# Expert weights in 4 MB transfers instead of 2 MB, in five places instead of ten

## What is computed

```python
logits = jnp.einsum('btd,de->bte', h, router_w)
affinity = jax.nn.softmax(logits, axis=-1)
gate, idx = lax.top_k(jnp.swapaxes(affinity, 1, 2), capacity)      # capacity = 32 tokens per expert
xe = jax.vmap(lambda hb, ib: hb[ib])(h, idx)
hidden = silu(einsum('becd,edf->becf', xe, w_gate)) * einsum('becd,edf->becf', xe, w_up)
ye = einsum('becf,efd->becd', hidden, w_down) * gate[..., None]
out[idx] += ye
```

## Time and profile before

| what | value |
|---|---|
| median of 3 runs | 1953.06 us |
| the profiled execution's own time | 1951.2 us |
| its span, first to last instruction | 1949.4 us |
| TensorE matmul busy | 1521.6 us, 78% |
| VectorE, ScalarE, GpSimd busy | 624.6, 526.5, 133.8 us |
| moved by DMA | 542.00 MB |
| expert weights | 192 transfers of 2048 KB, 46.0 to 46.6 us from issue to landing |

### The profile page before, as it was taken

The page is one execution under the profiler, slowest core; times in us unless marked ns, Lnnn a source line. Parts: engine busy times, 40 slices in busy tenths (PEclk is TensorE's granted clock), DMA queues, the critical chain, the costliest instruction groups (busy, mean ns, idle before and its releaser), DMA issues.

```text
span 1949.4 us, 25931 instructions
## 1 busy us (share of the span) xinstructions
PE 1521.6 (78%) x11219; PEld 1032.8 (53%) x11237; DVE 624.6 (32%) x963; ACT 526.5 (27%) x864; POOL 133.8 (7%) x151
## 2 busy tenths in 40 slices
PE   7999999999999997899888656556565655665555
PEld 7888999887999797789564111111111111111111
DVE  4665544665444554445752000000000000000000
ACT  6445343545343556425631000000000000000000
POOL 0251000031000013410200000000000000000000
PEclk9999999999999988999999787887778788787787
DMA  9443555433555443213097999999999999999997
GB/s 270 140 146 121 187 192 178 148 131 128 174 193 177 136 128 112 86 47 130 1 388 316 426 429 427 427 428 427 428 428 427 427 428 427 428 428 428 427 429 324
DMA packets 138528, 542.00 MB, mean 278 GB/s; under 512 B 10061, under 2 KB 103458, under 8 KB 113858
## 3 DMA queue, kind: packets, MB, share of 16 engines
q1 hardware_dynamic: 138386, 540.50, 70.5%
q0 software_dynamic: 48, 0.13, 0.0%
HBM read 539.56 MB, written 1.05 MB: 277 GB/s over the span
## 4 chain that ended last, share of the span: by engine, by line
PE 46%; DMA 43%; DVE 4%; ACT 3%; POOL 2%; issue 1%; SPq 0%; DVEq 0%; ACTq 0%; POOLq 0%
DMA ew<-in_expert_w_up_dram 14%; DMA ew<-in_expert_w_gate_dram 14%; DMA ew<-in_expert_w_down_dram 14%; PE bank L1049 12%; PE bank L1050 11%; PE bank L1051 11%; PE bank L1532 2%; POOL arena L670 1%; PE bank L1555 1%; ACT wH L713 1%; PE bank L1071 1%; PE bank L1133 1%; DVE wL L1576 1%; PE bank L1262 1%; PE bank L1056 1%
## 5 line engine op out<-in xcount | busy, mean ns | idle before, releaser
L1532 PE MATMUL bank<-ew,xeT 128*32 128x512 f32 x2048 | 344.5, 808 | 231.1 <-DMA ew<-in_expert_w_up_dram 123.5
L1576 DVE TENSOR_TENSOR wL<-ring,wH 128x2048 fp32r<-128x2048 f32 x128 | 295.3, 2307 | 285.9 <-ACT wH L713 285.6
L713 ACT ACTIVATE wH<-ring 128x2048 fp32r<-128x2048 f32 x128 | 244.1, 1907 | 310.1 <-PE bank L1051 307.7
L1532 PEld LDWEIGHTS bank<-ew,xeT 128*32 128x32 f32 x2048 | 65.1, 130 | 495.1 <-DMA ew<-in_expert_w_up_dram 207.4
L1049 PE MATMUL bank<-xH,wH 128*128 128x256 f32 x1056 | 303.5, 287 | 4.4 <-DVE wL L1576 4.2
L1050 PE MATMUL bank<-xL,wH 128*128 128x256 f32 x1056 | 300.1, 284 | 0.0
L1051 PE MATMUL bank<-xH,wL 128*128 128x256 f32 x1056 | 300.0, 284 | 0.0
L1555 PE MATMUL bank<-ew,tok 128*32 128x256 f32 x2048 | 164.6, 478 | 111.6 <-DMA ew<-in_expert_w_down_dram 105.4
L1049 PEld LDWEIGHTS bank<-xH,wH 128*128 128x128 f32 x1056 | 203.8, 193 | 10.4 <-issue 8.1
L1050 PEld LDWEIGHTS bank<-xL,wH 128*128 128x128 f32 x1056 | 204.0, 193 | 0.8
L1051 PEld LDWEIGHTS bank<-xH,wL 128*128 128x128 f32 x1056 | 203.8, 193 | 0.0
(11 more groups left out here) (280 smaller groups left out, 1786.8 us busy)
## 6 DMA issues: line engine op xcount, KB each, us to landing
ew<-in_expert_w_gate_dram SPq DMA_DIRECT2D x64, 2048.0 KB, 46.0
ew<-in_expert_w_up_dram SPq DMA_DIRECT2D x64, 2048.0 KB, 46.2
ew<-in_expert_w_down_dram SPq DMA_DIRECT2D x64, 2048.0 KB, 46.6
ring<-in_w_gate_up_dram SPq DMA_DIRECT2D x44, 1024.0 KB, 5.1
ring<-in_w_down_dram SPq DMA_DIRECT2D x22, 1024.0 KB, 4.9
ring<-in_w_in_dram SPq DMA_DIRECT2D x22, 1024.0 KB, 5.2
ring<-in_w_out_dram SPq DMA_DIRECT2D x12, 1024.0 KB, 4.9
ring<-in_w_in_fox_dram SPq DMA_DIRECT2D x10, 1024.0 KB, 8.9
```

Source lines behind the costliest of these rows:

```text
L713: act.activation(wH[:, n % 2, w], ring[:, slot(n), w], ACT.Copy).then_inc(w_hi, 1)
L1532: mm = pe.matmul(bank[half][32 * j:32 * j + 32, :], xeT[:, k, CAP * e:CAP * e + CAP], w_[:, m, 512 * j:512 * j + 512], start=(k == 0), sto ...
L1576: dve.tensor_tensor(wL[:, n % 2, w], ring[:, slot(n), w], wH[:, n % 2, w].bitcast(F32), ALU.subtract).then_inc(w_split, 1)
```

## The change

The units become 4 MB and the places 32 KB per partition: EU = 6, ESLOTS = 5, FIRST = 4. Gate and up are two units each, with four rows of the matrix in a partition, one run of 32 KB. Down is two units, each with two runs of 16 KB that lie 2 MB apart. The same memory holds five places; each of them is two of the old ones. The rows of a partition decide the channels of a block k, so the gather reads its stationary operand with a step of 4, and `ecols` is laid out to fit. e_used counts once per 4 MB.

```diff
-EU = 12
-ESLOTS = 10
-EW = 4096
+EU = 6
+ESLOTS = 5
+EW = 8192
-        EORDER = (0, 1, 2, 5, 3, 4, 6, 7, 8, 9)
+        EORDER = (0, 1, 2, 3, 4)
-            small(ecols[:, :].rearrange("p (u m) -> p u m", m=2),
-                  ffn_norm2.rearrange("l (u p m) -> p (l u) m", p=P, m=2))
+            small(ecols[:, :].rearrange("p (u m) -> p u m", m=4),
+                  ffn_norm2.rearrange("l (u p m) -> p (l u) m", p=P, m=4))
             def load_expert(e, u):
                 g = e * EU + u
-                if u < 8:
-                    src = (e_gate, e_up)[u // 4][0, e].rearrange("(u p m) f -> u p (m f)", p=P, m=2)[u % 4]
+                dst = ew[:, eslot(g), :]
+                if u < 4:
+                    src = (e_gate, e_up)[u // 2][0, e].rearrange("(u p m) f -> u p (m f)", p=P, m=4)[u % 2]
                 else:
-                    src = e_down[0, e].rearrange("(u p m) d -> u p (m d)", p=P, m=4)[u - 8]
-                sp.dma_start(ew[:, eslot(g), :], src).then_inc(e_full[eslot(g)], 16)
+                    src = e_down[0, e, 1024 * (u - 4):1024 * (u - 3), :].rearrange("(v p m) d -> p v (m d)", p=P, m=4)
+                    dst = dst.rearrange("p (v n) -> p v n", v=2)
+                sp.dma_start(dst, src).then_inc(e_full[eslot(g)], 16)
             sp.wait_ge(att["pv"], dif["pv"] + 16)
-            for g in range(3):
-                load_expert(0, g)
-            sp.wait_ge(w_split, NU - 4)
-            load_expert(0, 3)
+            load_expert(0, 0)
             sp.wait_ge(sn_ss, 4)
             sp.wait_ge(mTL, 4)
-            load_expert(0, 4)
+            load_expert(0, 1)
             sp.wait_ge(w_split, NU)
-            load_expert(0, 5)
-            load_expert(0, 6)
+            load_expert(0, 2)
             sp.wait_ge(w_used, NU)
-            load_expert(0, 7)
-            load_expert(0, 8)
+            load_expert(0, 3)
@@ scalar
-                act.wait_ge(e_used, e * EU + 4)
+                act.wait_ge(e_used, e * EU + 2)
@@ tensor, gather
-                            c0 = 2 * P * (k // 2) + k % 2
-                            mm = pe.matmul(b2(4 * part_ + k // 2)[:, k % 2, :], part[t][:, c0:c0 + 2 * P - 1:2],
+                            c0 = 4 * P * (k // 4) + k % 4
+                            mm = pe.matmul(b2(4 * part_ + k // 2)[:, k % 2, :], part[t][:, c0:c0 + 4 * P - 3:4],
@@ tensor, gate and up
-                    for u in range(4):
-                        if e in (0, NE // 2) and half == 0:
-                            pe.wait_ge((xe_ev, xe_evd)[u % 2], 8 * e // NE + u // 2 * 2 + 2)
-                        w_ = arrived(4 * half + u).rearrange("p (m f) -> p m f", m=2)
-                        for m in range(2):
-                            k = 2 * u + m
+                    for u in range(2):
+                        w_ = arrived(2 * half + u).rearrange("p (m f) -> p m f", m=4)
+                        for m in range(4):
+                            k = 4 * u + m
+                            if e in (0, NE // 2) and half == 0 and m % 2 == 0:
+                                pe.wait_ge((xe_ev, xe_evd)[m // 2], 8 * e // NE + 2 * u + 2)
@@ tensor, down
-                    w_ = arrived(8 + j).rearrange("p (m d) -> p m d", m=4)
+                    w_ = arrived(4 + j // 2).rearrange("p (v m d) -> p v m d", v=2, m=4)[:, j % 2]
-                    mm.then_inc(e_used, 1)
+                    if j % 2 == 1:
+                        mm.then_inc(e_used, 1)
@@ vector
-                dve.wait_ge(e_used, e * EU + 8)
+                dve.wait_ge(e_used, e * EU + 4)
```

## The result

The changed kernel takes 1961.19 us (median of 6 runs, 1959.49 to 1965.30) where the kernel before takes 1952.52 (6 runs beside it): ratio 1.0045, 95% interval 1.0034 to 1.0056, so 8.7 us slower. The profiled execution took 1960.66 us with a span of 1958.9.

A forecast was written before the change was run, and what follows sets the result against it. The second half, one stream of expert weights in 192 transfers of 2 MB, was taken as the bound. The terms 4.9 + 1.7 + 0.8 - 5.5 + 3.6 gave +5.5 us, 1958.6 us against the median, range 1948 to 1966.

The forecast's parts named there:

- likeliest case: Whole kernel: the summed terms hold, +5.5 us, own range 1954 to 1964, chance 0.42.
- One unit less ahead: Start of the stream: eight units' worth, not nine, filled before the experts start, costing +4.9 us.
- First release: Stream restart: the fifth transfer waits for four blocks of k instead of two, costing +1.7 us.
- Gather's strided load: Gather before the first release: TensorE's stationary operand loads with step 4 instead of 2, costing +0.8 us.
- Rival (e): Gather: weight loads double from 195 to 390 ns, all 32 seen, +10.9 us, 1964; chance 0.04.
- signs of being wrong: Stream: an interval under 9.76 or over 9.9 us, a second standstill, or a fifth issue outside 1036.3 to 1037.1.
- Rate of the stream: Expert weight stream: half as many gate and up packets, each 32 KB, save 11.4 ns apiece, -5.5 us.
- Rival (c): DMA engines: 32 KB runs are cut into 16 KB packets, +10.5 us, 1963.5; chance 0.10.
- (b): Stream: long runs remove its whole excess over the slope, with a fast tail, -4.7 us, 1948; chance 0.12.
- (d): Stream: paired runs or longer partition steps read worse; half a per cent gives +15 us, 1968; chance 0.10.
- rival (a): Whole sum: losses nearly cancel, high-clock tail, no gather price, full 6.6 us gain; +1.9 us, 1955; chance 0.22.
- Tail: Kernel end: the last arrival brings two quarters of down instead of one, slow start then recovery, +3.6 us.

The follow-up runs named there:

- e5: The kernel before with eight instead of nine 2 MB units loaded ahead of the experts: 1957.66 us, ratio 1.0030.
- e4: The changed kernel with gate and up also as 16 KB runs, so the gather keeps its old step of 2: 1962.73 us, ratio 1.0058.
- e2: The kernel before, still 2 MB transfers, with rows dealt to partitions as in the changed kernel, so the gather has step 4: 1955.20 us, ratio 1.0020.
- e1: The changed kernel with tokens written sorted by block of channels, so the gather's operands are contiguous: 1964.47 us, ratio 1.0059.
- e3: The changed kernel with its very last transfer cut into two of 2 MB, a semaphore each: 1958.16 us, ratio 1.0037.
- e9: As e7, but all units up to the eighteenth go singly instead of in pairs at the restart: 1949.60 us, ratio 0.9984.
- e7: The kernel before with 4 MB pairs mid-stream, gate and up in 32 KB runs, and tokens half sorted: 1950.85 us, ratio 1.0002.
- e8: The changed kernel with half-sorted tokens alone: 1960.42 us, ratio 1.0053.

## Why the prediction was right or wrong

The sign, the range and the likeliest case's mechanism were right: 1961.2 lies in 1948 to 1966, and slower by over 0.2% had 0.56. The size was +8.7 us where +5.5 was forecast, and nearly the whole difference is one term that was priced too low, the gather's. Point by point:

- **One unit less ahead, +4.9:** right. The changed kernel carries 92 transfers of 4 MB after the restart, and e5 gives 4.97 us in its profile for that alone.
- **First release, +1.7:** right, 3.71 against 1.98 us after expert 0's first matmul; e4 has 3.7 too (1033.0 to 1036.65). It was read from the trace and no run changed it alone.
- **Gather's strided load, +0.8:** this is the term that was mis-sized. Measured 3.7 us, shown by the changed kernel and e2 (a kernel of 2 MB transfers); with the old step (e4) or contiguous operands (e1) it is gone. The upper bound of 2.1 us was too low as well. It was taken from L1547, whose loads with the same step take 209 ns; but those are transposes, and the contiguous loads of that kind (L1541) take 143 and not 195 ns, so the row was one of another kind of load. A load's record grew by 137 ns here and not by 66. The records of neighbouring loads overlap, before and after, so what the gather pays is the interval between its products: it went from 4.02 / 32 = 0.126 us to 7.69 / 32 = 0.240, by 0.115 us. The Trainium skill's rule of two hits in a 16-byte line (SBUF — State Buffer, Specifications) had the direction. Read as a halving of the rate, as the prediction read it, it comes near if it is put on the interval, which grew 1.9-fold: 32 x 0.126 = 4.0 us for a measured 3.7. The prediction put it on the record of 195 ns, which grew 1.7-fold only, and so its 6.2 us were too much. Rival (e) named the mechanism, at too high a price, with a chance of 0.04. Of the signs of being wrong that the prediction named, one showed, and it is this term: the fifth issue came at 1040.60 us.
- **Rate of the stream, -5.5:** right in size. Measured -4.5 to -5.0, by a packet 9.4 to 10.4 ns (4.5 to 5.0 us / 480) in place of 11.4. e4 shows that it hangs on the runs; that it is a fixed price of a packet is argued from the agreement with the earlier trace rows and not shown apart. Rival (c) fell by the count of packets, rivals (b) and (d) by the interval of 9.80 us, rival (a) by the gather and by a tail that was not at the high clock.
- **Tail, +3.6:** right, 5.35 us against 1.93, +3.4, with a slow start and a recovery as forecast (granted clock 0.51 in the first 2 us, 0.78 after). e3 takes 1.8 of it away. The size is that of one execution: by the other profiles, one quarter at the end takes 1.9 to 3.5 us and two take 5.4 to 6.6.
- **Not foreseen:** gather(1) is longer too, so the seventh transfer went at 1055.37 and not 1047.3. The queue then still held what was issued at 1040.60 and 1044.03, so it cost nothing.

## What to carry to other kernels

Where a stream of transfers sets the end, price a coarser transfer by its edges: what is loaded ahead, the first release and the work behind the last byte. Here those were 10 us, while the gain of longer runs was 5, and mixing sizes (e9) kept most of the gain without these losses. A new layout in memory also moves the step with which other engines read, and one number of 4 bytes in every 16 was dear to all three engines that did it, while two of every four cost little (TensorE's step of 2, the copies in e7). A bound for a changed operand is to be taken from the same kind of instruction, and from the interval between instructions rather than from the length of one record, where records overlap.

## What the runs showed that was not expected

- ScalarE's copies of 128 x 1024 numbers with a source step of 16 bytes took 2.03 us each against 1.04, VectorE's 1.94 against 1.19; with runs of 8 bytes at a pitch of 16, in two instructions each, both engines took 1.32 us for the 1024 numbers.
- TensorE's weight load of 128 x 128 numbers in the gather took 192 ns contiguous, 195 with a step of 8 bytes, 332 with a step of 16 bytes, whatever the granted clock (0.75 to 1.00).
- The same work took different times by the granted clock from one profile to the next: the 17 products on zeros 4.75 us (e7) to 6.30 us (e8), the two quarters of down at the end 5.35 us (changed kernel) to 6.58 us (e4). That alone is more than several of the differences sought here.
